# A chunked delta-rule inverse in 64x64 diagonal pairs, with two smaller edits, in a hybrid attention block

## The reference, cut to what matters

```python
# gated delta rule, 4 heads of 128, per chunk of C tokens
gc = jnp.cumsum(g, axis=-1)
decay = exp(where(incl, gc[..., :, None] - gc[..., None, :], -inf))
lower = where(strict, einsum('cd,sd->cs', k * beta, k) * decay, 0.0)
t_inv = solve_triangular(eye + lower, eye)      # unit lower triangular inverse
u = t_inv @ (v * beta);  w = t_inv @ (k * beta * exp(gc))
attn = (q @ k.T) * decay
# scan over chunks: v_new = u - w @ state; o = q_dec @ state + attn @ v_new; state = ...
# stick breaking, 8 heads of 64
suffix = cumsum(log_sigmoid(-z), reverse=True) - log_sigmoid(-z)
a = exp(log_sigmoid(z) + suffix);  o = a @ v
```

## Time and profile before

| | |
|---|---|
| median of 3 runs | 2381.67 us (2379.85 to 2381.67) |
| profiled execution, its own time | 2382.03 us |
| its span | 2380.2 us |
| PE busy | 2340.7 us (98%) |
| weight loads of PE busy | 1917.6 us (81%) |
| DVE, ACT, POOL busy | 890.0, 771.4, 1283.1 us |

### The profile page before, as it was taken

How to read it: one execution, slowest core, us unless ns; L and a number is a source line. 1 busy time by engine, 2 the same in 40 slices (tenths; PEclk the granted TensorE clock), 3 DMA queues, 4 the chain that set the end, 5 groups by cost and what they waited for, 6 DMA issues and landing times.

```text
span 2380.2 us, 29590 instructions
## 1 busy us (share of the span) xinstructions
PE 2340.7 (98%) x11798; PEld 1917.6 (81%) x11798; DVE 890.0 (37%) x1404; ACT 771.4 (32%) x1537; POOL 1283.1 (54%) x732
## 2 busy tenths in 40 slices
PE   8999999999999999999999999999999999999998
PEld 7798877787877888888887988767778778888887
DVE  3653314343355431123356523243443445211233
ACT  5533325323136231122355442262140353211121
POOL 5511653564553566677655126635555535666774
PEclk9999999999999999999999999999999999999999
DMA  4300331332231333333223013313322313333331
GB/s 152 98 27 28 89 89 53 98 89 72 79 100 44 106 107 97 98 98 98 80 77 89 19 36 91 87 47 113 89 80 71 93 49 95 119 98 97 97 95 66
DMA packets 105753, 196.84 MB, mean 83 GB/s; under 512 B 8464, under 2 KB 18832, under 8 KB 105360
## 3 DMA queue, kind: packets, MB, share of 16 engines
q1 hardware_dynamic: 104464, 188.65, 26.2%
q10 hardware_dynamic: 1152, 6.29, 0.8%
HBM read 192.82 MB, written 2.10 MB: 82 GB/s over the span
## 4 chain that ended last, share of the span: by engine, by line
PE 91%; DVE 5%; ACT 3%; issue 1%; DMA 0%; DVEq 0%; ACTq 0%
PE big L1686 66%; PE mix L1686 9%; PE mix L1824 5%; DVE c_lo L1429 1%; PE big L2000 1%; PE mix L1968 1%; PE mix L1894 1%; PE mix L2069 1%; PE mix L1979 1%; PE mix L1787 1%; PE mix L2201 1%; PE mix L2150 0%; DVE scr L1441 0%; PE mix L1741 0%; PE mix L2134 0%
## 5 line engine op out<-in xcount | busy, mean ns | idle before, releaser
L568 POOL TENSOR_SCALAR ring_hi<-stage 128x1024 fp32r<-128x1024 f32 (+3 forms) x364 | 372.1, 1022 | 1042.6 <-PE big L1686 962.2
L570 POOL TENSOR_TENSOR ring_lo<-stage,ring_hi 128x1024 fp32r<-128x1024 f32 (+3 forms) x364 | 912.6, 2507 | 30.4
L1686 PE MATMUL big<-h_hi,ring_hi 128*128 128x512 f32 (+1 forms) x1888 | 720.3, 382 | 2.8 <-DVE h_lo L1149 1.5
L1686 PE MATMUL big<-h_hi,ring_lo 128*128 128x512 f32 (+1 forms) x1888 | 709.9, 376 | 0.0
L1686 PE MATMUL big<-h_lo,ring_hi 128*128 128x512 f32 (+1 forms) x1888 | 709.9, 376 | 0.0
L1686 PEld LDWEIGHTS big<-h_hi,ring_hi 128*128 128x128 f32 x1888 | 355.7, 188 | 75.3 <-issue 9.0
L1686 PEld LDWEIGHTS big<-h_lo,ring_hi 128*128 128x128 f32 x1888 | 355.6, 188 | 65.4
L1686 PEld LDWEIGHTS big<-h_hi,ring_lo 128*128 128x128 f32 x1888 | 355.8, 188 | 63.8 <-issue 1.9
L1628 DVE TENSOR_TENSOR h_lo<-scr,h_hi 128x1024 fp32r<-128x1024 f32 x64 | 84.7, 1324 | 248.4 <-ACT h_hi L1067 248.4
L1686 PE MATMUL big<-ring_hi,h_hi 128*128 128x512 f32 x448 | 174.5, 391 | 0.0
L1686 PE MATMUL big<-ring_lo,h_hi 128*128 128x512 f32 x448 | 174.3, 391 | 0.0
(11 more groups left out here) (292 smaller groups left out, 2826.3 us busy)
## 6 DMA issues: line engine op xcount, KB each, us to landing
stage<-in_w_in SPq DMA_DIRECT2D x168, 512.0 KB, 3.5
stage<-in_w_mlp_in SPq DMA_DIRECT2D x64, 512.0 KB, 3.6
stage<-in_w_mlp_out SPq DMA_DIRECT2D x64, 512.0 KB, 3.8
stage<-in_w_o SPq DMA_DIRECT2D x16, 512.0 KB, 3.8
stage<-in_w_br_a SPq DMA_DIRECT2D x8, 512.0 KB, 3.8
stage<-in_w_br_c SPq DMA_DIRECT2D x8, 512.0 KB, 3.8
stage<-in_w_br_d SPq DMA_DIRECT2D x8, 512.0 KB, 3.9
stage<-in_w_br_b SPq DMA_DIRECT2D x8, 512.0 KB, 3.5
```

Of the source, the lines that this page charges most:

```text
L568: nc.gpsimd.tensor_scalar(rH[jw][0:pp, r, 0:kk, 0:job.n], w, 1.0, 0.0, ALU.mult, ALU.add).then_inc(sem("w_hi"), 1)
L570: nc.gpsimd.tensor_tensor(rL[jw][0:pp, r, 0:kk, 0:job.n], w, f32(rH[jw][0:pp, r, 0:kk, 0:job.n]), ALU.subtract).then_inc(sem("w_ready"), 1)
L1686: ins_ = MM(o_, a_, r_, start=s0, stop=s1)
```

## The change

Four things change. (1) The inverse is done for the two 64x64 diagonal blocks of each 128x128 matrix side by side in levels 1 to 5: rows 0 to 63 hold one block, rows 64 to 127 the other. Level 6 is one 64x64 corner: Y = corner x T, X = transposed Y x U. T, the masked matrices and the lower copies are half as wide, V is a product with a slice of the identity instead of a transposition, and all four heads of one e share one tile, where two heads did. (2) R and B come from two products of 256 columns each in float32r, from a tile `g_rows` that holds gates and betas as split rows (a new step "gt": two products turn them, four DVE operations split them). (3) `gc` moves one unit ahead, `decays(0)` into the middle of the last unit of `av`; for b > 0 DVE does `scores_out` and `first_level` ahead of `row_decays`. (4) At p = 3, ACT copies the first gate tile ahead of two exponentials.

```diff
@@ ScalarE
+                if p == 3:
+                    gate_c_copy(p, (0,))
                 for e in range(2):
                     act.wait_ge(*upto("c_sum", place(sum_order, p, 3 + e)))
                     stick_weights(p, e)
-                gate_c_copy(p)
+                gate_c_copy(p, (1,) if p == 3 else range(2))
@@ VectorE
+            for e in range(2):
+                rows, cols = slice(32 * e, 32 * e + 16), slice(e * P, (e + 1) * P)
+                TS(g_rows[rows, cols], ps[rows, cols], 1.0, None, ALU.mult).then_inc(sem("a_rhi"), 1)
...
+                i = TT(g_rows[low, cols], ps[rows, cols], f32(g_rows[rows, cols]), ALU.subtract)
...
-                TT(pairs(ps), pairs(ps), g_dec[e], ALU.mult).then_inc(sem("a_lt"), 1)
-                dve.wait_ge(*upto("a_lt", b + 1))
-                TT(g_LTm[e], ps, per_mask(consts[:, CLV + P:CLV + 2 * P]), ALU.mult).then_inc(sem(f"a_LTm{e}"), 1)
+                for rows in HALVES:
+                    TT(ps[rows, :, rows], ps[rows, :, rows], g_dec[e][rows, :, rows], ALU.mult).then_inc(sem("a_lt"), 1)
+                TT(blocks(g_LTq[e]), ps[0:HB, :, HB:P], g_dec[e][0:HB, :, HB:P], ALU.mult).then_inc(sem("a_ltq"), 1)
+                for q, rows in enumerate(HALVES):
+                    dve.wait_ge(*upto("a_lt", 2 * b + q + 1))
+                    i = TT(blocks(g_LTm[e])[rows], ps[rows, :, rows], level(1, rows), ALU.mult)
+                i.then_inc(sem(f"a_LTm{e}"), 1)
@@ TensorE
-                per_head_tile(("R", b), lambda o_, h: MM1(o_, s_g[:, b, h:h + 1].to_broadcast((P, P)), triu))
-                per_head_tile(("B", b), lambda o_, h: MM1(o_, s_be[:, b, h:h + 1].to_broadcast((P, P)), ident))
+                for name, row in (("R", 8), ("B", 0)):
+                    ps = tile_of((name, b))
+                    for q in range(2):
+                        at = CROW - CRD + row + 2 * b + q
+                        i = MM1(ps[:, 2 * P * q:2 * P * (q + 1)], rot_r[:, at:at + 1].to_broadcast((P, P)), g_rows[:, :])
+                    done(i, (name, b))
...
-                            for q in range(2):
-                                i = MM1(ps[:, q * P:(q + 1) * P], g_LTm[e][:, 2 * c + q, :], g_T(e, 2 * c + q))
+                        for h in range(GH):
+                            if n < LEVELS - 1:
+                                for rows in HALVES:
+                                    i = MM1(ps[rows, h * HB // 2:(h + 1) * HB // 2], blocks(g_LTm[e])[rows, h, :],
+                                            level_half(blocks(g_T[e])[rows, h, :], n, 0))
+                            else:
+                                i = MM1(ps[HB:P, h * HB:(h + 1) * HB], blocks(g_LTq[e])[:, h, :], blocks(g_T[e])[0:HB, h, :])
...
-                                for q, h in enumerate((2 * c, 2 * c + 1)):
-                                    i = TR(ps[:, q * P:(q + 1) * P], g_T(e, h), ident)
+                        for h in range(GH):
+                            for rows in HALVES:
+                                one = ident[rows, rows] if n == LEVELS - 2 else level_half(ident[rows, rows], n, 1)
+                                w = HB if n == LEVELS - 2 else HB // 2
+                                i = MM1(ps[rows, h * w:(h + 1) * w], blocks(g_T[e])[rows, h, :], one)
```

More of the change, by code:

```diff
@@ L92, in shape_constants @@
     levels = []
-    for n in range(7):
-        z = 1 << n
-        levels.append(one((c // (2 * z) == p // (2 * z)) & (c % (2 * z) >= z) & (p % (2 * z) < z)))
+    for n in range(6):
+        z, q, r = 1 << n, p % HB, np.arange(HB)[None, :]
+        levels.append(one((r // (2 * z) == q // (2 * z)) & (r % (2 * z) >= z) & (q % (2 * z) < z)))
     k = np.arange(2 * P)[None, :]
@@ L284, in mixer_keys @@
             for t in "YXV" if n < LEVELS - 1 else "YX":
-                k += [(t, b0 + e, n, c) for e in range(2) for c in range(2)]
+                k += [(t, b0 + e, n) for e in range(2)]
         for b in (b0, b0 + 1):
@@ L1219, in level_mask, with level @@
                 e = b % 2
[L1220 to L1223, removed]
+                mix_wait(dve, ("Y", b, n - 1))
+                TT(blocks(g_LTm[e]), blocks(g_LT[e]), level(n), ALU.mult).then_inc(sem(f"a_LTm{e}"), 1)
             def per_mask(ap):
                 return ap.unsqueeze(1).to_broadcast((P, GH, P))
+            def level(n, rows=slice(0, P)):
+                return consts[rows, CLV + n * HB:CLV + (n + 1) * HB].unsqueeze(1).to_broadcast((rows.stop - rows.start, GH, HB))
             if l == 0:
@@ L1349, in natural_k_v @@
                 mix_free(TT(g_vb, heads(ps), per_head(s_be[:, b, :]), ALU.mult), ("vn", b))
+            for e in range(2):
+                V.memset(g_U[e][HB:P, :, 0:HB], 0.0).then_inc(sem("a_S0"), 1)
             exponents(0)
@@ L1843, in tensor_layer @@
             do("aab")
-            do("av", between=value_unit)
+            for i in range(3):
+                unit(JOB["av"], i)
+                value_unit(i)
+            unit(JOB["av"], 3, (0, 1))
+            decays(0)
+            unit(JOB["av"], 3, (2, 3))
             set_fill("gatea0", "az")
@@ L1859, in tensor_layer @@
                     mix_freed(pe, ("LT", b0 + e))
-                    per_head_tile(("T0", b0 + e), lambda o_, h: TR(o_, g_U(e, h), ident))
+                    ps = tile_of(("T0", b0 + e))
+                    for h in range(GH):
+                        for rows in HALVES:
+                            i = MM1(ps[rows, h * HB:(h + 1) * HB], blocks(g_V[e])[rows, h, :], ident[rows, rows])
+                    done(i, ("T0", b0 + e))
                 natural_k_v(b0)
@@ L1887, in tensor_layer @@
[L1887 to L1895 removed]
+                        key = ("Y", b0 + e, n)
@@ new lines, in tensor_layer @@
+                        done(i, key)
+                    for e in range(2):
+                        key = ("X", b0 + e, n)
+                        ps = tile_of(key)
+                        mix_freed(pe, ("Y", b0 + e, n))
+                        if n > 1:
+                            mix_freed(pe, ("V", b0 + e, n - 1))
+                        for h in range(GH):
+                            if n < LEVELS - 1:
+                                for rows in HALVES:
+                                    at = slice(h * HB // 2, (h + 1) * HB // 2)
+                                    i = MM1(ps[rows, at], blocks(g_V[e])[rows, h, :], g_Yc[e][rows, at])
+                            else:
+                                i = MM1(ps[0:HB, h * HB:(h + 1) * HB], blocks(g_Yq[e])[:, h, :], g_U[e][HB:P, h, HB:P])
+                        done(i, key)
```

194 lines of the change are left out of this document (106 added, 88 removed), and 10 rows, old and new, of the table PER_LAYER.

## The result

The changed kernel takes 2395.39 us (median of 14 runs, 2378.02 to 2408.63) against 2380.83 us before (14 runs, 2378.97 to 2382.43): a ratio of 1.0063, 95% interval 1.0048 to 1.0078, so 14.6 us slower. The forecast was 2356, range 2346 to 2400, with 0.71 for faster. The median lies in the range; the sign is wrong. The spread is a result too: 31 us, where the kernel before has 3.5, and each run's time follows its mean granted clock (2378.02 at 0.989, 2395 to 2402 at 0.975 to 0.979, 2408.63 at 0.972). The profiled execution is the slowest: 2408.63, span 2406.8.

The account below looks back on a forecast made before the run. PE was taken as the bound, busy for 98% of the span and carrying 91% of the last-ending chain. The terms summed to -26.4 us, 2382.0 to 2355.6, stated as 2356, range 2346 to 2400.

Parts of the forecast that it names:

- the sum: Whole kernel: -29.3 + 2.0 + 0.4 - 5.2 + 5.0 + 3.2 - 2.5 = -26.4 us, 2382.0 to 2355.6.
- the clock falls: Rival, levels: clock drops to 0.50 as little of the array works; 2411 us, chance 0.21, of it 0.06 in part only.
- Part 1, the levels: Inverse: row halves run side by side, 0.031 us an instruction; block 18.6 against 25.9, -29.3 us for four blocks.
- mode switches: Around the levels: changing from full to quarter tiles empties the array, four changes a block at 0.12 us, +2.0 in all.
- The serial rival: Levels: the halves do not run side by side, 0.063 us an instruction, level 6.0, block 34; 2417 us, chance 0.06.
- Part 2, R and B: R and B products: 0.5 us a chunk instead of 1.8; 1.3 less, counted for chunks 2 and 3, -5.2 us.
- Part 3, the front: Ahead of the first block: later DVE chain, some 5 us of PE standing, net 2.5 a layer, +5.0 (0 to +10).
- the upper bound: Ahead of the first block: +10 us if a slow row decay now falls ahead of the masks of level 2.
- Chunks 2 and 3: DVE's chain on the path at the T0s and X of level 1: 1.6 us a layer, +3.2 (0 to +6).
- Part 4, the gate: Earlier ACT gate copy removes PE's 1.27 us stand in both layers: -2.5 us, 0 at worst.
- longer waits: Rival, blocks: a slow DVE operation in each block and 3.8 us a level; 2372 us, chance 0.14.
- a clock that falls in part of the blocks: Rival, inverse: half clock in only some blocks gives 2370 to 2400 us, chance 0.06.

Follow-up runs that it names:

- 64 columns: Changed kernel with the 32 moving columns of its 64-row products (levels 1 to 5) moved twice over, 64 in one instruction: 2371.94 us, ratio 0.9965.
- without edits 2 and 3: Changed kernel with parts 2 and 3 taken back, inverse and gate copy kept: 2363.97 us with 64 moving columns, 2382.26 with 32.
- 64 columns, banks put right: Changed kernel with columns moved twice over, and R of chunk 0 on gt's bank so later tiles keep their earlier banks: 2365.89 us, ratio 0.9943.
- 128 columns: Changed kernel with the 32 moving columns of its 64-row products moved four times over, 128 in one instruction: 2406.29 us, ratio 1.0111.
- the run with chunk 0's order changed: Changed kernel with VectorE doing scores and first level ahead of row decays for chunk 0 too: 2388.04 us, ratio 1.0033.
- the run with split rows for chunks 1 to 3: Inverse and gate copy, columns moved twice over, B of chunk 1 used early, R and B from split rows for chunks 1 to 3: 2358.80 us.

## Why the prediction was wrong, point by point

- **The step that failed: the sum has every level at full clock, with no term for the clock, and gave the rival "the clock falls" 0.21 against 0.57.** The argument against the rival was that the levels of before kept 1.00, half of their products with 64 columns. But the new products move 32, and the runs show that this is what separates the cases: with 64 repeated the clock holds in every block, with the same instructions, loads and stands. It cost 23.4 us with all edits, 18.3 without edits 2 and 3. The rival had the mechanism, but its price, +55, was more than twice too high: it took half clock as 0.062 a product where 5.12/96 is 0.053, and let it last 3.6 levels in every block, where the start of the fall moves from run to run.
- **Part 1, the levels, was right.** Forecast 3.2 a level and 18.6 a block, and 0.5 for mode switches; measured at full clock 3.13 to 3.18 a level and 20.3 to 20.6 a block, where before took 26.9 and 27.6: 6.6 and 6.9 less, against 7.3 less 0.5 for the changes of array mode (6.8). The copy of 128 columns took 277 ns (forecast 276). The halves run side by side, 0.029 for each instruction. The serial rival is out.
- **Part 2, R and B: the size was right (0.48 us of PE's stream from 95.94 to the next unit, forecast 0.5), the list of consequences was not.** The new inverse has 248 mixer tiles a layer (316 before), a multiple of the four banks either way; gt makes 249. The round of banks then starts layer 2 on the bank that layer 1 ends on; PE stood 4.13 us at the boundary, and 6.05 is what undoing it gave by the medians. The sum had no term for it. No row of before shows it; counting the tiles in the code does.
- **Part 3, the front: mis-sized.** Forecast +2.5 a layer; measured 7.48 at level 1, and 5.23 with 64 columns, where the half clock behind the stand lasted 3.4 us and not 6.8. In the 7.48 stand 4.67 for the stand ahead of the lower product of chunk 1 (the forecast had "some 5" for all stands, and there are 0.95 and 1.18 more), 1.7 for that product at half clock (119.85 to 123.29, where 1.72 is its time before) and 1.2 for the start of the unit behind it at half clock; the small stands and savings about cancel. The slow row decay of the earlier trace rows did not vanish: it moved from chunk 1 to chunk 0, ahead of the use of B. I had a slow row decay only in the upper bound; it is a collision with a weight split of GpSimd that both traces show (the split runs from 117.86 to 120.63 before, from 111.26 to 113.66 after).
- **Chunks 2 and 3:** from block to block before takes 31.44; the new inverse without edits 2 and 3 takes 34.24 (64 columns, 147.64 to 181.88 in its timeline), and with them 32.74. So the new inverse, through VectorE's longer chain, costs 2.8 a layer (forecast 1.6, bound 3.0), and R and B give 1.5 of their 2.6. The waits are behind line 1362, the first level, which itself waits 0.83 for ACT's two half copies.
- **Part 4, the gate: right.** -2.5 forecast, -2.6 measured alone, and the wait of twice 1.27 is gone from the trace.
- **The sum.** Without the clock and the boundary the kernel takes 2365.89 (64 columns, banks put right), 14 us under before where the forecast had 26. The 10 us between 2355.6 and it are those of the two mis-sized parts: 5.23 for 2.5 at the front, and from block to block 32.74 - 31.44 = 1.3 where 1.6 - 2.6 = -1.0 was forecast; together 5.0 in layer 1, and twice that if layer 2 does the same (an estimate). That 2395.39 lies in the stated range says nothing for the sum, whose own bounds were 2346 to 2366: the range was widened to 2400 for longer waits and a clock that falls in part of the blocks.

## What to carry over

When an edit replaces products by more and smaller ones, price it at both levels of the clock, and ask how many columns each instruction moves, not whether PE stays busy: here 64 moving columns cost hardly more than 32 and kept the clock. Count what a new tile does to a rotation of banks as far as its next wrap. A slow elementwise operation in the trace may be a collision; see what the other engine runs beside it before the edit moves it. And look for the price of a moving column in the trace, by type: the rate of plain float32 stood in the trace of before.

## What the runs showed of the hardware

- The clock fell to 0.50 and stayed there with PE busy all of the time, in stretches of 64-row products of 32 moving columns 0.029 us apart (13 of 16 blocks), and in none of 36 blocks with 64 or 128 columns. It falls at no fixed place (1.7 to 14.2 us into a block over these runs), and the times of the 14 runs, 31 us apart, follow their mean clock. The Trainium skill, "TensorE: Matmul & The Clock Gate", section "Why this matters for your kernels", asks that there be no long idle gaps between bursts of products; by that rule the blocks would have stayed at 1.00, and the rows at 193.40 show 0.50 with no gap.
- A moving column of plain float32 took 0.84 ns at full clock (0.429 us for 512), one of float32r about half of that (0.23 us for 512), and products on two parts of the array shared the time: a pair of 128 columns took 0.109, as one on the whole array does.
- A VectorE operation on two SBUF operands took 2.90 us instead of 0.68 when it started beside a GpSimd split on SBUF, and a copy of only 128x4 took 1.96 instead of 0.17; VectorE's operations with an operand in PSUM kept their time beside such a split (0.69 at 110.48 in the run with chunk 0's order changed, where the split runs from 109.78 to 112.18). From the run with split rows for chunks 1 to 3:

```profile
109.81 1.96 DVE L1377 COPY st<-scr 128x4 f32<-128x4 f32 x1
109.33 2.41 POOL L584 TENSOR_TENSOR ring_lo<-stage,ring_hi 128x1024 fp32r<-128x1024 f32 x1
```

The Trainium skill, "SBUF — State Buffer", section "SBUF: two separate sides", says that the two engines share one pair of ports, which a VectorE operation with two SBUF inputs or in a two-port mode, or one of GpSimd, holds for its whole instruction if it starts first. The rows agree: the copy ends as the split does (111.77 and 111.74), the row decay 0.54 behind it (114.20 and 113.66).
